# A four-layer mixer decoder step on eight cores: the order of the first pass, its loads, and the place of the sample sums

## What is computed

```python
def trunk_layer(x, ...):
    h = rmsnorm(x, pre_g)
    u, v, z_a, p, z_b, xc, bg, cg, z_c = split(h @ w_in)      # 768x3, 512x2, 768x4 columns
    a_out, vn = chunk_gmlp(u, v, v_g, w_s, b_s)                # u * (W_s[h] @ rmsnorm(v) + b), chunks of 128
    b_out, new_pool = pool_mixer(p, pool_buf, ...)             # window means 2/4/8/16 - p, then a 128x128 product
    c_out, new_conv = short_conv(xc, bg, cg, conv_buf, conv_w) # bg * conv3(cg * xc)
    mix = concat([a_out * silu(z_a), b_out * silu(z_b), c_out * silu(z_c)])   # 2048
    out = mix @ w_out
    return x + rmsnorm(out, post_g), new_pool, new_conv, vn
```

## Time and profile before

| | us |
|---|---|
| three runs | 2032.94, 2039.46, 2148.82 |
| median | 2039.46 |
| the profiled execution | 2033.48 |
| its span, slowest core | 2032.3 |
| spans of the eight cores | 2029.0 to 2032.3 |

### The profile page before, as it was taken

One profiled execution on the slowest core, in us unless ns is written; L12 is line 12 of the kernel. 1 busy time (PEld: TensorE's weight loads), 2 busy tenths in 40 slices (PEclk: granted clock), 3 DMA queues, 4 the chain that ended last, 5 costly groups with the idle time before them and its releaser, 6 DMA issues.

```text
span 2032.3 us, 37323 instructions; the slowest of 8 cores (2029.0 to 2032.3 us)
## 1 busy us (share of the span) xinstructions
PE 2004.1 (99%) x12305; PEld 1185.9 (58%) x12305; DVE 1174.8 (58%) x1935; ACT 630.7 (31%) x1566; POOL 382.7 (19%) x752
## 2 busy tenths in 40 slices
PE   7999999999999999999999999999999999999998
PEld 4555565576566466557656546656755655664673
DVE  4654764575665475476575556547657544653763
ACT  4232332323323232232332332323333222231331
POOL 3211310221211120131131122013013111101300
PEclk9999999999999999999999999999999999999999
DMA  9999797689798875839969857595987974656662
GB/s 187 215 193 193 167 204 105 171 131 193 178 181 139 161 157 94 138 115 181 183 169 177 137 156 145 96 140 135 194 186 168 160 144 137 115 87 144 115 122 75
DMA packets 157099, 309.53 MB, mean 152 GB/s; under 512 B 78192, under 2 KB 83568, under 8 KB 155504
## 3 DMA queue, kind: packets, MB, share of 16 engines
q0 software_dynamic: 47376, 174.64, 54.5%
q1 hardware_dynamic: 109392, 132.25, 23.7%
q10 hardware_dynamic: 144, 0.26, 0.0%
HBM read 409.48 MB, written 55.99 MB: 229 GB/s over the span
## 4 chain that ended last, share of the span: by engine, by line
PE 93%; DMA 4%; DVE 1%; issue 1%; POOL 0%; SPq 0%; ACT 0%; DVEq 0%; POOLq 0%; ACTq 0%
PE ps L590 61%; PE ps L706 23%; PE ps L558 7%; DMA hd<-sb_hout 2%; DMA sb_b_bc<-b_sp 1%; PE ps L829 1%; DMA sb_ring<-w_in 1%; DMA sb_xs<-x_p 1%; PE ps L684 1%; PE ps L747 0%; DVE sb_pw L410 0%; DVE sb_mix L414 0%; POOL sb_stats L425 0%; DVE sb_vn L414 0%; ACT sb_scr L406 0%
## 5 line engine op out<-in xcount | busy, mean ns | idle before, releaser
L590 PE MATMUL ps<-sb_hT,sb_ring 128*128 128x384 bf16 (+1 forms) x8448 | 1324.7, 317 | 6.6 <-DVE sb_mix L414 3.0
L590 PEld LDWEIGHTS ps<-sb_hT,sb_ring 128*128 128x128 bf16 x8448 | 823.1, 98 | 471.6 <-issue 12.1
L406 ACT ACTIVATE sb_scr<-ps 128x384 f32<-128x384 f32 (+3 forms) x665 | 370.8, 562 | 1047.2 <-PE ps L590 494.2
L706 PE MATMUL ps<-sb_wout,sb_mix 128*128 128x512 bf16 x2144 | 464.7, 379 | 0.0
L706 PEld LDWEIGHTS ps<-sb_wout,sb_mix 128*128 128x128 bf16 x2144 | 209.9, 98 | 251.6
L356 POOL DMA_DIRECT2D sb_ring<-w_in x284 | 153.3, 543 | 973.1 <-PE ps L590 626.2
L414 DVE SCALAR_TENSOR_TENSOR sb_scr<-sb_pw,sb_convw,sb_scr 128x384 f32<-128x384 f32 (+1 forms) x336 | 182.0, 542 | 145.8 <-ACT sb_ccarry L406 109.5
L410 DVE TENSOR_TENSOR sb_scr<-ps,sb_scr 128x384 f32<-128x384 f32 (+1 forms) x288 | 151.8, 531 | 118.2 <-PE ps L829 91.4
L414 DVE SCALAR_TENSOR_TENSOR sb_hout<-sb_xs,sb_stats,sb_pre_bc 128x1024 bf16<-128x1024 f32 x62 | 79.6, 1285 | 189.3 <-POOL sb_stats L425 168.7
L558 PE MATMUL ps<-sb_ring,sb_hT 128*128 128x512 bf16 (+1 forms) x1088 | 178.8, 326 | 0.9 <-DMA sb_ring<-w_in 0.9
L410 DVE TENSOR_TENSOR sb_mix<-sb_scr 128x384 bf16<-128x384 f32 (+1 forms) x288 | 160.2, 556 | 30.7 <-DVE sb_scr L410 0.9
(11 more groups left out here) (55 smaller groups left out, 521.5 us busy)
## 6 DMA issues: line engine op xcount, KB each, us to landing
sb_ring<-w_in POOLq DMA_DIRECT2D x273, 512.0 KB, 10.9
xd<-sb_xs SPq DMA_DIRECT2D x51, 512.0 KB, 3.1
sb_xs<-xd SPq DMA_DIRECT2D x51, 512.0 KB, 11.8
sb_xs<-x_p SPq DMA_DIRECT2D x32, 512.0 KB, 15.2
sb_wout<-w_out POOLq DMA_DIRECT2D x32, 512.0 KB, 13.0
hd<-sb_hout SPq DMA_DIRECT2D x62, 256.0 KB, 4.2
sb_ring<-w_in POOLq DMA_DIRECT2D x11, 1024.0 KB, 9.9
y_p<-sb_xs SPq DMA_DIRECT2D x16, 512.0 KB, 2.9
```

Source lines behind the costliest of these rows:

```text
L406: return emit(ACT, lambda a: a.activation(out=out, in_=in_, func=func, scale=scale, **kw), reads=reads, writes=writes)
L590: ins = pe.matmul(bank(b, N), lhsT=wa.ap[:, k, :], rhs=hT[:, k, j0 * 128:j0 * 128 + N], start=(k == 0), stop=(k == 7))
L706: ins = pe.matmul(bank(b + half), lhsT=mix[:, k, j * 128:(j + 1) * 128], rhs=wout[:, k, half * 512:(half + 1) * 512], start=(k == 0), stop ...
```

## The change

Four things are changed.

1. The first pass. Its order becomes p, three convolution heads, v, gating heads, the other three convolution heads, and the ring's list has the weights in that order. All six first row tiles are issued at once; tiles 4 and 5 go to the space of the last two output weight pieces. The first ring load is issued behind the first norm, not ahead of it. VectorE copies the transposed tiles. The small constants, the v gain and four row tiles of the next pass are issued once p's weights are there. The pooling windows of this pass start behind the third convolution head.
2. The output weights of the first pass are issued behind heads 1 and 2 of the convolution, behind v tiles 1, 3 and 5, and behind gating heads 0 to 2; until all eight are issued, no ring load of a later pass is (`hold`).
3. Sample passes. The sample chains go to GpSimd (`pool_vec_sample`), from a list `side` of their own, in place on the stage buffer of the v state; the gating heads take nothing from `later`, since VectorE's prompt chains are through by then.
4. Smaller ones: a third hout buffer (`NHO`), the bias without its copy for samples (read with a stride of zero), and in `out_last` EPS is added to the first half's sum early, and the sums no longer wait for the multiply of VectorE.

```diff
-NHO = 2
+NHO = 3
+N_FRONT = 3
...
+        hold = []
             u = pending[0]
+            if hold and u.l + u.g > 0:
+                return False
...
+            if (g, l) == (0, 0):
+                k = len(units) - 12
+                units = units[:2] + units[k:k + 2 * N_FRONT] + units[2:k] + units[k + 2 * N_FRONT:]
+            pending.extend(units)
...
-            act(hT[:, :, j * 128:(j + 1) * 128], pb.rearrange("p (k t) -> p k t", k=8), AF.Copy,
-                reads=[bank_res[b]], writes=[R_hT[j]])
+            if on_dve:
+                dve_copy(hT[:, :, j * 128:(j + 1) * 128], pb.rearrange("p (k t) -> p k t", k=8),
+                         reads=[bank_res[b]], writes=[R_hT[j]])
+            else:
...
+        side = []
+
+        def side_pop(n):
+            for _ in range(min(n, len(side))):
...
+        def pool_vec_sample(srs, R_src, dv, R_d, w):
+
+            n0, n = 15 * SB, 128
+            cur, R_cur, off, k, i = srs, R_src, 0, 1, 0
+            while k < w:
+                ext = (w - 2 * k) * SB
+                a, ln = n0 - ext, n + ext
+                o, i0, i1 = (bufs[i][:, 0:ln], cur[:, a - off:a - off + ln],
+                             cur[:, a - off - k * SB:a - off - k * SB + ln])
+                side.append(lambda o=o, i0=i0, i1=i1, r_=R_cur: emit(
+                    POOL, lambda q: q.tensor_tensor(out=o, in0=i0, in1=i1, op=ALU.add), reads=[r_], writes=[R_v]))
+                cur, R_cur, off = bufs[i], R_v, a
+                i ^= 1
+                k *= 2
+            sm = cur[:, n0 - off:n0 - off + n]
+            side.append(lambda: emit(POOL, lambda q: q.tensor_scalar(out=sm, in0=sm, scalar1=1.0 / w, scalar2=None,
+                                                                     op0=ALU.mult), reads=[R_v], writes=[R_v]))
+            side.append(lambda: emit(POOL, lambda q: q.tensor_tensor(out=dv, in0=sm, in1=srs[:, 15 * SB:23 * SB],
+                                                                     op=ALU.subtract),
+                                     reads=[R_v, R_src], writes=[R_d]))
...
-                srs = pbs[:, gi, :]
-                sv2, R_s2 = window_ops(srs, 15 * SB, 128, SB, w, R_pbs[gi])
-                later.append(lambda: dve_stt(dv[:, Np:Np + 128], sv2, 1.0 / w, srs[:, 15 * SB:23 * SB],
-                                             ALU.mult, ALU.subtract, reads=[R_s2, R_pbs[gi]], writes=R_d))
+                pool_vec_sample(pbs[:, gi, :], R_pbs[gi], dv[:, Np:Np + 128], R_d[1], w)
...
-                dve_tt(scr[:, tm + half, :], bank(b + half), post_bc[:, half * 512:(half + 1) * 512], ALU.mult,
-                       reads=[bank_res[b + half], R_stat[sa[half]], R["post_bc"]], writes=[R_scr[tm + half]])
+                summed = R_stat[sa[half]].w
+                emit(DVE, lambda v, half=half: v.tensor_tensor(
+                    out=scr[:, tm + half, :], in0=bank(b + half), in1=post_bc[:, half * 512:(half + 1) * 512],
+                    op=ALU.mult),
+                     reads=[bank_res[b + half], R["post_bc"]], writes=[R_scr[tm + half]], extra=[summed])
+                if half == 0:
+                    emit(POOL, lambda q: q.tensor_scalar(out=c0, in0=c0, scalar1=EPS, scalar2=None, op0=ALU.add),
+                         reads=[R_stat[sa[0]]], writes=[R_stat[sa[0]]])
             emit(POOL, lambda q: q.tensor_tensor(out=c1, in0=c1, in1=c0, op=ALU.add),
                  reads=[R_stat[x] for x in sa], writes=[R_stat[sa[1]]])
-            rs = rstd_from(sa[1])
+            emit(POOL, lambda q: q.tensor_tensor(out=c1, in0=c1, in1=neghalf[:], op=ALU.pow),
+                 reads=[R_stat[sa[1]], R["neghalf"]], writes=[R_stat[sa[1]]])
+            rs = c1
...
-                        bv = b_bc[:, k, h * 128:(h + 1) * 128]
+                        bv = b_bc[:, h * 128:(h + 1) * 128]
-                        if m > 1:
+                        if k == 1:
+                            bv = bv[:, 0:ST].unsqueeze(2).to_broadcast([128, ST, SB])
...
-                later_pop(2 if h == 0 else 3)
+                if g < 2:
+                    later_pop(2 if h == 0 else 3)
...
-        def c_phase(g, l, hook):
+        def c_phase(g, l, hook, c0=0, c1=6):
-            for c in range(6):
+            for c in range(c0, c1):
...
-                emit(SP, lambda s_: s_.dma_start(out=icnt[:].rearrange("p a b -> p (a b)"), in_=icnt_d),
-                     writes=[R["icnt"]], dsem=d_icnt)
-                sl = [load_x(0, 0)]
+                spare = [wout[:, 2 * k:2 * k + 2, :].rearrange("p k d -> p (k d)").bitcast(F32) for k in (6, 7)]
+                def load_first(k):
+                        sl = load_x(0, k)
+                        return xs[:, sl, :], R_xs[sl]
+                    emit(SP, lambda q: q.dma_start(out=spare[k - NX], in_=x_p[k * 128:(k + 1) * 128, :]),
+                         writes=[R_wout[k + 2]], dsem=d_first[k - NX])
+                    return spare[k - NX], R_wout[k + 2]
+                rows = [load_first(0)]
                 load_pre(0)
-                sl += [load_x(0, 1), load_x(0, 2), load_x(0, 3)]
+                rows += [load_first(k) for k in range(1, GT)]
...
-                ring_try_alloc()
                 warm_up()
                 nr(0)
+                ring_try_alloc()
                 nr(1)
-                ring_try_alloc()
-                sl.append(load_x(0, 4))
                 tj(0, 8)
                 nr(2)
-                load_wpg(0, 1, d_wpg[0])
                 ring_try_alloc()
-                sl.append(load_x(0, 5))
                 nr(3)
-                ring_try_alloc()
                 tj(2, 4)
-                load_vg(0)
                 nr(4)
+                ring_try_alloc()
                 nr(5)
+                ring_try_alloc()
                 pump()
+                load_wpg(0, 1, d_wpg[0])
...
-                tj(4, 0)
                 pb_[2] = p_matmul(g, l, 2, 0)
+                tj(5, 0)
-                tj(5, 0)
...
+                pw_ = wsched[(g, l)][("p", 3)].res[0].w
+                SP.h.wait_ge(*pw_)
+                SP.waited[id(pw_[0])] = pw_[1]
+                setup_loads()
+                emit(SP, lambda s_: s_.dma_start(out=icnt[:].rearrange("p a b -> p (a b)"), in_=icnt_d),
+                     writes=[R["icnt"]], dsem=d_icnt)
+                load_vg(0)
                 for gi in range(4):
-                    pj(gi, 1)
+                    p_job(g, l, gi, 1)
                     release(wsched[(g, l)][("p", gi)])
+                R_w32 = [R_vn[4], R_vn[5]]
+                wo = hold
+                wo.extend(range(8))
+
+                def hook(c):
+                    if c == 0:
+                        emit(SP, lambda q: q.dma_start(out=w32, in_=w_sp[0]), writes=R_w32, dsem=d_pw[1])
+                        load_b(0)
+                    else:
+                        wout_piece(l, wo.pop(0))
+                    if c == 1:
+                        dve_tt(wmt[:], w32.rearrange("p (a b) -> p a b", a=6),
+                               c32[:, C32_MASKP, :].unsqueeze(1).to_broadcast([128, 6, 128]), ALU.mult,
+                               reads=R_w32 + [R["c32"]], writes=[R["wmt"]])
+                c_phase(g, l, hook, 0, N_FRONT)
+                for gi in range(4):
                     pool_vec(g, l, gi)
-                    later_pop(2 if gi else 0)
-                v1 = W0["v1"].res[0].w
-                SP.h.wait_ge(*v1)
-                SP.waited[id(v1[0])] = v1[1]
-                setup_loads()
-                w32 = mix[:, 10:12, :].rearrange("p k t -> p (k t)").bitcast(F32)
-                R_w32 = R_mix[10] + R_mix[11]
-                emit(SP, lambda q: q.dma_start(out=w32, in_=w_sp[0]), writes=R_w32, dsem=d_pw[1])
-                load_b(0)
...
                     elif i > 2:
                         later_pop(2 if g == 2 else 1)
+                        side_pop(2)
...
-            wo = list(range(8)) if g == 0 else []
+            if pi:
+                wo = list(range(8)) if g == 0 else []
...
-                if wo and j in ((3, 5) if pi == 0 else (1, 3, 5)):
+                if wo and j in (1, 3, 5):
                     wout_piece(l, wo.pop(0))
-                if j >= 3 or nt - j <= 3:
+                if (j < 4 if pi == 0 else j >= 3 or nt - j <= 3):
                     init_load()
-                later_pop(2 if g == 2 else 1)
+                if g < 2:
+                    later_pop(1)
+                elif j < nt - 1:
+                    later_pop(1)
+                    side_pop(4)
...
-                if wo and h % 2 == 1:
+                if wo and (h % 2 == 1 or pi == 0):
...
-                if c == 1 and (g == 0 or pi == 1) and l + 1 < DEPTH:
+                if c == (1 if pi else N_FRONT) and (g == 0 or pi == 1) and l + 1 < DEPTH:
...
-            c_phase(g, l, hook)
+            c_phase(g, l, hook, 0 if pi else N_FRONT)
```

50 lines of the change are left out of this document (29 added, 21 removed).

## The result

Six executions of the changed kernel took 2052.94 to 2055.79 us, median 2053.98; the median of the six executions of before is 2033.71. The ratio is 1.0096, 95% interval 1.0083 to 1.0109: 20 us slower, 6.2 us above the forecast of 2047.8. (One disturbed execution of before, 2148.82 us, is left out of this ratio; later comparisons leave such executions out too.)

The account below looks back on a forecast made before the run. TensorE was taken as the bound (busy 2004.1 of 2032.3 us), with DMA the second limit in the first pass. 2033.5 - 6.5 (first pass) + 22.0 (sample passes) - 1.2 (tail) = 2047.8 us; own range 2038 to 2058, 8-in-10 range 2021 to 2063.

Parts of the forecast that it names:

- Sample passes: Four sample passes: 22.0 us lost, 6.0 in each of layers 0 to 2 and 4.0 in the last; bounds 14 and 36.
- the hindrance between the engines: Sample passes: VectorE and GpSimd hold each other up, raising a pass's loss from 4.1 towards 8 us; 6.0 taken, midway.
- Ten of them with gaps of 0.15 are 6.9 us: Sample pass: ten GpSimd sums ahead of tile 0's root take 6.9 us, two ring issues 1.1, ending at 403.1.
- the floor of 4.1: Sample pass of a layer: 4.1 us lost as lower bound, if the two engines don't hinder each other.
- First pass: First pass: 6.5 us won, output matmuls at 161.2 after a new 4.3 us wait in head 5; bounds 1.5 and 11.8.
- such a wait lowers the clock, 1.0 us: First pass, head 5: the new 4.3 us wait for weights lowers TensorE's clock, costing 1.0 us.
- no wait at v: First pass: a sign that the forecast is right, TensorE not waiting at v, which now follows three convolution heads.
- rival (4): First pass: front load of output weights makes v or head 3 late, only 1.5 us won, 2053 us; chance 0.08.
- Tail: Behind the last matmul: the final multiply starts at 2024.8 instead of 2025.96, 1.2 us won; bounds 0.8 and 1.3.
- (1): Sample passes: GpSimd sums are hidden, nothing lost and 3.3 us of waits go, 2022.5 us; chance 0.22.
- (2): Sample passes: full exclusion of the two engines and a lower clock behind each long wait, 2062 us; chance 0.16.
- (3): First pass: the weight stream keeps up and 11.8 us are won, the rest as forecast, 2042.5 us; chance 0.10.

Follow-up runs that it names:

- hout3b: The kernel before with a third hout buffer and the bias row shared by prompt and samples, nothing else; ratio to before 0.9984.
- sums_alone: The kernel before with only the sample sums put on GpSimd, in the changed kernel's order; ratio to before 1.0136.
- sums_spread: The changed kernel with the same eighteen GpSimd sums a pass, five instead of ten ahead of tile 0's root; ratio to before 1.0005, median 2036.9 us.
- no_sums: The changed kernel without the eighteen GpSimd sums of each sample pass, VectorE's window sums kept; 2027.43 us, one execution.
- no_next_rows: sums_vec without the six row loads for the second pass (3.1 MB left out); ratio to before 0.9927.
- no_windows: The changed kernel without VectorE's ten window additions of each sample pass, the four closing operations still run; 2045.98 us, one execution.
- sums_vec: The changed kernel with the sample sums back on VectorE in the order of before; ratio to before 0.9975.
- loads_late: sums_vec with the calls for the second pass's first row loads moved behind the fourth v tile; three of four still left early; ratio to before 0.9968.

## Why the prediction was right, and where it was off

The forecast had the sign, the mechanism and the place; 2053.98 lies in its own range of 2038 to 2058. That the total came so near is in part the range: the two large terms were mis-sized, by 3.6 and 4.5 us, both the same way, and there was room for it.

- **Sample passes: 22.0 forecast, 25.6 measured.** Layers 0 to 2 lost 23.0 and not 18.0, the last layer 2.6 and not 4.0. Right: a wait before the fifth v tile in three passes of four and two in the first head (there in all four). The term that was too small is the hindrance between the engines, 1.9 of the 6.0. "Ten of them with gaps of 0.15 are 6.9 us", with the issues 8.0, holds for sums that nobody disturbs; beside VectorE it was 10.8, with the ten at 8.1 by themselves (1.29, 0.80, 0.45, 0.79, 0.72, 0.78, 0.61, 0.93 and twice 0.88) where the prices make 5.3. So the first wait was 4.4, not 1.7. The roots of tiles 1 and 2, forecast for 409.1 and 412.9, ended at 409.5 and 413.4; since the pass started 2.2 us earlier, they were 2.6 and 2.7 us late, not on time. If the floor of 4.1 holds, which no run shows, the rest was 3.6 a pass; what the runs do show of it is the 2.8 us of stretch ahead of the first root and 0.9 us for the last vn behind a window step. The two waits in the first head are other ones than forecast: 1.7 for the bank of tile 2 and 0.6 for the last vn; the one for tile 1's bank was covered by the slow fifth tile. And "the 2.3 us of 1088 elements" is 2.6 of 1216, which moves nothing.
- **First pass: 6.5 forecast, 2.0 measured.** Most steps held on the profiled core: second half-columns of p at about 27.2 (forecast 27.8), no wait near 100, a wait of 3.8 in the last head (4.3). The 4.5 us are two terms: the last head's weights were there at 155.7, not 153.3, and "such a wait lowers the clock, 1.0 us" was 2.9. "no wait at v" was wrong too, 2.9 us and 1.2 us of slower clock; how far it held up the last head's weights, whose ring slots come free behind it, isn't separated. Above these lies that the sum took one core for eight: the mean core won 8.3 us, more than forecast, and the slowest had about rival (4)'s 1.5.
- **Tail: 1.2 forecast, 1.2 measured.** hout3b and sums_alone keep the old tail (2.2 us between the starts of the last two VectorE operations); the changed kernel and its variants have 1.05.
- **Rivals.** (1), hidden sums, failed where it was said to be decided: vn of tile 0 ended at 406.1, not before 404.1. sums_spread shows that it was near at hand: the order of the sums decided it. VectorE's windows, on which the text had it rest ("ten steps of 0.8 use it up"), do use it up: 1.3 us of wait in no_sums. But the first heads gave that back, and it cost 0.3 us in all. (2), over 1.5 us a window step, did not show. (3), a stream that keeps up, held for three cores of eight as far as the first outputs; (4) fits the slowest.

What stays open: why one core's v weights come 3 to 5 us later than another's in the same execution. The runs show that it goes with volume, and not which shared part of the path makes it. No run holds all early row loads back while still doing them, which would need a wait of SP.

## What to carry to other kernels

Before work is moved to an engine that is idle most of the time, look at what short operations it has on someone's path: they wait behind the new work in the queue. Ten sums ahead of one root and four ahead of each of the next two cost 26 us in four passes here, where the fourteen operations on VectorE had cost nothing that shows (154.4 us a pass with them, 154.5 without). The same work spread between the roots cost a quarter. And where all cores load at full DMA share, read the stage on every core: a reordering that wins 8 us on average can win 2 on the slowest. Less volume was worth more here than any change of order (10 us, no_next_rows). And before a run with moved loads is read, look in the trace where they were issued: a call that stands later in the program is not a later issue if its queue has nothing to wait for.

## What was not expected of the hardware

- Eight cores with the same program drift apart by 11 us in 167 when their loads are dense (155.3 to 166.7), and by 3 before; with 3 MB less it is 2 us.
- A GpSimd add of 128x128 took 1.29 us in both the changed kernel and no_windows while VectorE's multiply of 128x1024 (1.46 us, 1.29 in sums_vec) ran, and others of its size took 0.44 to 0.72. Both are stretched, so the engines do hinder each other, but not fully: ten sums and ten window steps, 5.3 and 7.0 us alone, were through in 10.8 us with two issues among them.
- Behind a wait of 3.8 us TensorE lost 2.9 us more to the clock, in the 48 matmuls that followed (10.88 for 7.96 us); behind 5.0 us in loads_late it was 2.5 (10.45). These two waits cost 1.8 and 1.5 times their length. In the sample passes the lower clock behind a wait of 4.4 us was covered by the next wait and cost next to nothing.
